# First stage of a two-block transformer kernel: the place of x in the load order, the sum of its squares, and its turned copy

## The reference, cut to what matters

```
mod = silu(c) @ w_mod + b_mod                 # six vectors of 1024; sh1, sc1 are the first two
mod_c = silu(c_ctx) @ w_mod + b_mod           # the same for the context
hx = rmsnorm(x, g_mix) * (1 + sc1) + sh1      # rmsnorm: x * rsqrt(mean(x*x) + eps) * g
hc = rmsnorm(ctx, g_mix) * (1 + csc1) + csh1
q, k, v, gates, o = hx @ w_in, and the same of hc   # four heads of 128
...                                           # chunked mLSTM over both, read-out, y
x = x + ga1 * y                               # x is needed again, by rows (tokens)
```

## Time and profile before

| | us |
|---|---|
| median of 3 runs | 1362.35 (1361.59 to 1362.79) |
| profiled execution | 1360.7 |
| its span in the profile | 1358.8 |
| PE busy | 1338.1 (98%) |
| DVE busy | 1122.8 (83%) |
| ACT busy | 779.3 (57%) |

### The profile page before, as it was taken

How to read it: one execution, slowest core, us unless ns; L and a number is a source line. 1 busy time by engine, 2 the same in 40 slices (tenths; PEclk the granted TensorE clock), 3 DMA queues, 4 the chain that set the end, 5 groups by cost and what they waited for, 6 DMA issues and landing times.

```text
span 1358.8 us, 18999 instructions
## 1 busy us (share of the span) xinstructions
PE 1338.1 (98%) x7406; PEld 1155.9 (85%) x7406; DVE 1122.8 (83%) x1659; ACT 779.3 (57%) x1145; POOL 12.9 (1%) x28
## 2 busy tenths in 40 slices
PE   8999999999999999999999999999999999999998
PEld 5988978888878888889878888888888897888886
DVE  7978787998989988879789888889887798796652
ACT  7722857676376555474475555476553757755542
POOL 0000000000000000000000000000000000000000
PEclk9999999999999999999999999999999999999999
DMA  9778445865949878777449879768889652575561
GB/s 377 285 241 302 152 157 188 297 245 199 381 185 325 298 285 330 299 259 272 165 182 329 291 287 335 292 244 319 296 283 386 218 202 93 220 264 190 192 217 33
DMA packets 64936, 343.57 MB, mean 253 GB/s; under 512 B 7408, under 2 KB 9920, under 8 KB 36688
## 3 DMA queue, kind: packets, MB, share of 16 engines
q1 hardware_dynamic: 62448, 335.35, 67.7%
q0 software_dynamic: 2224, 6.86, 1.5%
q10 hardware_dynamic: 176, 0.16, 0.0%
HBM read 341.25 MB, written 1.09 MB: 252 GB/s over the span
## 4 chain that ended last, share of the span: by engine, by line
PE 89%; DVE 4%; ACT 3%; DMA 2%; issue 1%; SPq 0%; ACTq 0%; DVEq 0%
PE bank L336 88%; DMA raw<-w_stream 2%; ACT T L836 1%; ACT rstd L738 1%; PE bank L693 1%; DVE wlo L332 1%; DVE X L930 0%; ACT whi L301 0%; PE bank L1136 0%; DVE SGC L911 0%; DVE wlo L287 0%; ACT whi L275 0%; DVE XN L871 0%; PE bank L2495 0%; DVE QR L2338 0%
## 5 line engine op out<-in xcount | busy, mean ns | idle before, releaser
L336 PE MATMUL bank<-hh,whi 128*128 128x512 f32 (+1 forms) x2160 | 484.6, 364 | 1.2 <-ACT SGC L1209 0.5
L332 DVE TENSOR_TENSOR wlo<-raw,whi 128x2048 fp32r<-128x2048 f32 x197 | 450.1, 2287 | 35.3 <-ACT whi L301 35.2
L301 ACT ACTIVATE whi<-raw 128x2048 fp32r<-128x2048 f32 x197 | 376.8, 1915 | 128.7 <-DMA raw<-w_stream 79.7
L336 PEld LDWEIGHTS bank<-hh,whi 128*128 128x128 f32 x2160 | 380.4, 189 | 60.9 <-issue 1.8
L336 PE MATMUL bank<-hh,wlo 128*128 128x256 f32 x1896 | 289.4, 283 | 0.0
L336 PEld LDWEIGHTS bank<-hh,wlo 128*128 128x128 f32 x1896 | 261.4, 191 | 8.2
L336 PE MATMUL bank<-whi,hid_hi 128*128 128x512 f32 x440 | 172.0, 391 | 0.0
L336 PE MATMUL bank<-wlo,hid_hi 128*128 128x512 f32 x440 | 171.3, 389 | 0.0
L336 PE MATMUL bank<-whi,hid_lo 128*128 128x512 f32 x440 | 171.3, 389 | 0.0
L1026 DVE SCALAR_TENSOR_TENSOR mring<-mring,con 128x1024 f32<-128x1024 f32 x107 | 130.2, 1220 | 15.7 <-DMA mring<-m_stream 15.7
L1223 ACT ACTIVATE GU<-bank 128x512 f32<-128x512 f32 x100 | 59.1, 591 | 104.8 <-PE bank L336 104.8
(11 more groups left out here) (344 smaller groups left out, 1418.6 us busy)
## 6 DMA issues: line engine op xcount, KB each, us to landing
raw<-w_stream SPq DMA_DIRECT2D x217, 1024.0 KB, 5.5
mring<-m_stream SPq DMA_DIRECT2D x139, 512.0 KB, 5.0
cb<-m_stream SPq DMA_DIRECT2D x53, 512.0 KB, 5.6
con<-gate_rows POOLq DMA_DIRECT2D x8, 512.0 KB, 7.1
raw<-w_stream SPq DMA_DIRECT2D x4, 512.0 KB, 7.4
con<-const_d SPq DMA_DIRECT2D x1, 1472.0 KB, 14.9
XF<-xT SPq DMA_DIRECT2D x1, 1024.0 KB, 13.3
XC<-ctxT SPq DMA_DIRECT2D x1, 1024.0 KB, 10.1
```

What stands on the lines that cost most here:

```text
L301: nc.scalar.activation(w_hi(c, 0, CW), raw[:, c % RAW_SLOTS], ACT.Copy).then_inc(s_hi, 1)
L332: nc.vector.tensor_tensor(w_lo(c, 0, CW), raw[:, c % RAW_SLOTS], w_hi(c, 0, CW).bitcast(f32), ALU.subtract).then_inc(s_lo, 1)
L336: return nc.tensor.matmul(out, lhsT, rhs, start=start, stop=True, skip_group_check=True)
```

## The change

x is loaded after chunk 7 instead of after chunk 3, and the 128 KB of constants before chunk 4. ACT rounds all of chunks 0 to 7, then squares x, then makes its two `mrow` copies, then rounds the first half of chunk 8, then makes rstd. DVE no longer adds the squared tiles: PE sums all eight of them, after chunk 7. Only then does PE turn `mrow`, now into bank 6, and after it all four groups of x, into banks 0, 1, 2 and 6. The filler products go. The turned x is copied to `X` later: two groups on ACT behind chunk 10's rounding, two on DVE behind the rests of chunk 9.

```
-            pe.wait_ge(s_pair, 1)
-            for j in range(2):
+            for j in range(DT):
+                if j % 4 == 0:
+                    pe.wait_ge(s_sq, j + 4)
                 ins = mm(bank[7][:, 0:SEQ], ones, SQF[:, j], j == 0)
...
-            pe.wait_ge(s_ln, 1)
+            pe.wait_ge(s_in[6], 16)
+            pe_first_stat(pe)
             for g in range(4):
...
             ins.then_inc(s_mT, 1)
-            turn_x(3)
-            pe.wait_ge(s_xc, 3)
-            pe_fill(pe, 3, ident, XF[:, 0], 4)
+            pe.wait_ge(s_in[3], 16)
+            for n in range(4):
+                if n == 3:
+                    pe.wait_ge(s_mm0, 1)
+                turn_x(n)
             pe_first_chunks(pe, U["x1"], c)
...
             dve_half_rest(dve, c, 1)
             dve_halves(dve, c + 1)
+            for n in range(2, 4):
+                dve.wait_ge(s_xt, n + 1)
+                nc.vector.tensor_copy(xrow(*GROUPS[n]), bank[X_BANKS[n]][:]).then_inc(s_xc, 1)
...
             chunks(0, 4)
-            sp.dma_start(XF[:], xT).then_inc(s_in[3], 16)
             sp.dma_start(con[:, 0:2 * P], const_d[:, 0:2 * P]).then_inc(s_in[6], 16)
             chunks(4, 8)
+            sp.dma_start(XF[:], xT).then_inc(s_in[3], 16)
```

More of the change, by code:

```diff
@@ L545, in pe_ctx_stat @@
         def pe_ctx_stat(pe):
-            pe.wait_ge(s_pair, 2)
+            pe.wait_ge(s_pair, 1)
             for j in range(2):
@@ L1370, in turned_bank @@
             return bank[3 if h < HEADS - 1 else 4]
-        X_BANKS = (4, 5, 6, 0)
+        X_BANKS = (0, 1, 2, 6)
         s_zero = sem("zeros_set")
@@ L1394, in pe_lstm @@
             for k in range(DT):
[L1395 to L1400, removed]
                 for g in range(4):
@@ L1412, in pe_lstm @@
                 for m in range(4 * g, 4 * g + 4):
-                    ins = nc.tensor.transpose(bank[7][:, SEQ + 4 * m:SEQ + 4 * m + 4], mrow[:, m * P:(m + 1) * P],
+                    ins = nc.tensor.transpose(bank[6][:, 4 * m:4 * m + 4], mrow[:, m * P:(m + 1) * P],
                                               ident[0:4, 0:4])
             ins.then_inc(s_mT, 1)
-            turn_x(3)
-            pe.wait_ge(s_xc, 3)
-            pe_fill(pe, 3, ident, XF[:, 0], 4)
+            pe.wait_ge(s_in[3], 16)
[3 more added lines that the diff above has]
+                turn_x(n)
             pe_first_chunks(pe, U["x1"], c)
@@ L1436, in pe_lstm @@
             pe.wait_ge(s_lo, c + 3)
-            pe.wait_ge(s_mm0, 1)
             gates(1, hhi, hlo)
+            pe.wait_ge(s_xc, 4)
             keys(0, 0)
@@ L1449, in values @@
                 pe_wide(pe, c + 5 + j, 4 * (j % 2), [bank[b + 4 * (j // 2)][:] for b in range(4)], his, los)
-            pe.wait_ge(s_xc, 4)
             values(0)
@@ L1559, in x_tokens @@
                 nc.scalar.activation(xrow(t, h), bank[X_BANKS[n]][:], ACT.Copy).then_inc(s_xc, 1)
-            for j in range(4):
+            for j in range(DT):
                 halves_of(j)
             act_first_squares(act)
[L1564 to L1570, removed]
             for g in (2, 3):
@@ L1573, in act_lstm @@
                 nc.scalar.activation(mrow[:, g * 512:(g + 1) * 512], bank[g][0:4], ACT.Copy).then_inc(s_mrow2, 1)
+            act_first_half(act, c)
+            act_rstd(act, N_X1, D)
             act_second_half(act, c)
@@ L1577, in act_lstm @@
             act_split(act, c + 2)
+            x_tokens(0)
+            x_tokens(1)
             act_squares(act, N_CTX, lambda j: XC[:, j], lambda j: (s_in[2], 16), False)
@@ L1582, in act_lstm @@
             act_split(act, c + 4)
-            x_tokens(3)
             act.wait_ge(s_in[4], 16)
@@ L1705, in dve_lstm @@
                 dve_halves(dve, j)
[L1706 to L1709, removed]
             for g in range(2):
@@ L1716, in dve_lstm @@
             nc.vector.tensor_reduce(CG[:, 0:2 * FIRST_MODS],
-                                    bank[7][:, SEQ:SEQ + 4 * FIRST_MODS].rearrange("p (m t) -> p m t", t=2), AX.X, ALU.add)\
+                                    bank[6][:, 0:4 * FIRST_MODS].rearrange("p (m t) -> p m t", t=2), AX.X, ALU.add)\
                 .then_inc(s_mm0, 1)
```

## The result

Over 22 runs each, the changed kernel takes 1364.04 us (1361.82 to 1366.93) and the one before 1361.88 us (1359.61 to 1366.28). The ratio is 1.0016, with a 95% interval of 1.0010 to 1.0022: 2.2 us slower (1.4 to 3.0), inside the 0.2% (2.7 us) that I called no change, though the end of the interval is not. The forecast was 1365.0 us, 2.65 us over the median then known. Two runs further down lie far off the others of their kernels and are left out of medians and ratios: one of ten of e1 (4722.94 us) and one of eight of e2 (1468.86 us, granted clock 0.85).

What follows compares the result with a forecast made beforehand. PE was taken to bound the kernel, unbroken from 43.43 us, so first-stage delays carry to the end. 1.4 + 1.2 = 2.6 us; median 1362.35 + 2.65 = 1365.0 us, own range 1364.4 to 1365.6, overall 1362.2 to 1366.8.

Steps and rivals of the forecast that it cites:

- What bounds: Whole program: PE bounds it, without a gap from 43.43 us, so a shift of that start carries to the end.
- The stream: Loads of the first stage: chunk 8 lands at 30.6 again, chunks 4 to 7 come 2.5 us sooner, x at 27.5.
- First term: First modulated tile on ACT: +1.4 us, as PE's eight sums of squares (sixteen passes) now lie on the path.
- Second term: DVE before the gates: two copies of x delay chunk 10's rest, +1.2 us, a PE gap of about 1.1 us.
- Rival A: At the gates: DVE's copies are hidden and PE does not wait for chunk 10; 1363.8 us, chance 0.11.
- Rival B: At chunk 8: early weights let rstd follow its first half on ACT without idling, DVE's copies hidden; 1362.3 us, chance 0.10.
- Rival C: Sums on PE: they run at the lower clock level, passes at double spacing, 3.3 us more; 1368.3 us, chance 0.07.
- two signs: Evidence against the lower clock on PE: spacing stayed short after an idle 0.84 us, and the granted clock was 1.00.
- Rival D: Loads: x lands beside chunk 8, later than its place in line; at 30.6, +1.5 us, 1366.5 us, chance 0.06.
- slower by over 0.2%: Whole run: over 2.7 us slower, chance 0.39, from 0.28 of the forecast's own spread with C and D.

Runs made afterwards that it cites:

- e1: The changed kernel with DVE's two copies of the turned x made by ACT behind chunk 11's rounding; 1364.29 us, ratio 1.0014 to the kernel before.
- e2: The changed kernel with DVE adding the squares pairwise, so PE sums four tiles instead of eight; 1364.02 us, ratio 1.0014 to the kernel before.
- the first experiment: The same run as e1: DVE's two copies of x given to ACT in the changed kernel; 1364.29 us, ratio 1.0014 to the kernel before.
- e10: The kernel before with only ACT's list reordered, its load order kept; 1361.94 us, ratio 0.9999 to the kernel before.
- e7: The changed kernel with ACT's two copies of x moved behind chunk 11's rounding, DVE's two left; one run, gates 20.78 us after chunk 8.

## Why the prediction was right

- **What bounds, and that the shift is carried on: right.** 2.35 us at the gates, 2.35 us at 221 us.
- **The stream: right.** x at 27.58 (27.5 said), chunk 8 again at 30.6, chunk 6 at 22.47 (22.5), and PE at the sums at 29.30 (29.4).
- **First term: right, a little large.** 1.26 us measured, 1.4 said (the working gives 33.05 + 0.9 - 32.52 = 1.43). A pass cost 0.216 us (0.217), the sums ended 0.1 us sooner since PE began 0.1 sooner, and ACT took 0.83 us from the start of L562 to its next instruction, not 0.9. The doubled sums showed that every pass is on the path.
- **Second term: right in size, incomplete in cause.** 1.09 us measured, 1.2 said; two copies on DVE did take 1.20 us, and 0.1 of it filled the wait for ACT's squares that stood there before. The "gap of about 1.1 us" in PE was counted from the start that the gates could have had (49.56 + 0.76 = 50.32, by the kernel before); the profile's 0.82 us counts from the end of the last pass (50.59). The prediction said that ACT's two copies leave the context's squares done at 47.1, "still ahead of the pair sums". That held, with 0.1 us to spare, and it meant more than I wrote: this was a second hold of nearly the same length, the one that had been last before. Asking what would be late next if DVE's copies were not there would have shown it, and the expectation of the first experiment would not have failed.
- **Rival A** (copies hidden) fell at the gap of 0.82 us. **Rival B**: its bound held. With four sums ACT went from 30.42 to 32.19 without idle time, 0.14 us sooner against chunk 8 than before, and nothing more was to be had until ACT's list was reordered, which it had taken as given. **Rival C**: the passes were 0.216 us apart. Of the two signs that the prediction named, only this spacing decides. The granted clock reads 1.00 at the sums, but it reads 1.00 from 8 to 12 us too, where the products of 512 columns start 0.43 us apart, against 0.23 later. That early stretch, the two ahead of the sums and that of the sums (span, busy time per engine, then PEclk):

```profile
8.00:12.00 4.00, 3.65 (x8) 2.48 (x8) 2.68 (x4) 2.23 (x3) 0.00 (x0) 1.00 1.01 426
24.00:28.00 4.00, 3.84 (x15) 2.22 (x14) 4.00 (x4) 2.79 (x4) 0.00 (x0) 1.00 1.04 422
28.00:29.30 1.30, 1.30 (x6) 0.86 (x5) 1.30 (x3) 1.30 (x2) 0.00 (x0) 1.00 0.99 410
29.30:33.00 3.70, 3.70 (x20) 3.00 (x18) 1.31 (x2) 2.34 (x5) 0.00 (x0) 1.00 1.01 423
```

  By the rule of the Trainium skill ("TensorE: Matmul & The Clock Gate", "HAM oscillation — how this bites in real kernels") this rival was not the likely one, as the prediction had it: the page's case is a wait for the next load that is longer than the burst of products before it. The trace shows no such wait here: PE was busy for 3.84 of the 4 us from 24 to 28, and its longest wait between chunks from 12 us to the sums was 0.50 us. **Rival D**: x landed in its turn.
- **The time.** 2.65 us was said, 2.2 (1.4 to 3.0) measured, 2.35 in the trace. The absolute figure was another 0.5 us high because the median of the first three runs (1362.35) lay above that of 22 (1361.88). The time alone would not have told the forecast from rival A: 2.2 us lies between A's 1.4 and the 2.65 said, and the interval reaches both. It is the gap at the gates that rules A out.
- **Chances.** The terms given for "slower by over 0.2%" add up to 0.28 + 0.07 + 0.06 = 0.41 with C and D taken whole, not 0.39.

## What to carry to other kernels

Work that runs under a stream of loads is free only there. Moving an operand to the end of the stream puts everything made of it on the path, so its reduction has to be short by then: eight float32 sums on TensorE cost 1.3 us where four, with two additions on another engine, cost nothing. Before a copy is put on an engine, ask not only what is queued behind it but which other engine's list, moved by the same edit, ends 0.1 us behind it: a hold that is hidden by another shows no wait in the profile until that one is taken away. And a shift of 2 us in a run of 1360 is read in the trace from a fixed event (here the landing of a load), not from two spans.

## What was not expected of the hardware

The wait for the same load on the path, some 1060 us into the program, took 6.20, 8.13, 8.22, 7.20, 6.91, 6.61, 5.62, 7.06, 6.82, 6.96, 7.44 and 6.82 us in the twelve profiles (before, changed, e1 to e10), with no relation to the edit: e1 with 8.22 and e7 with 6.82 differ only in how x is copied at 45 us. Waits of 6.1 to 7.7 us for weights at about 372, 563 and 867 us, and of 7.4 to 8.8 us for `m_stream` at 359 to 364, lay on the path in some of the profiles and not in others. Between the two fixed places (at about 221 and 1185 us) the twelve profiles take 960.3 to 964.2 us: 3.9 us, nearly twice the effect of the change. And the landing of chunk 8, at the end of 30 us of unbroken transfers, varied by 0.3 us (30.33 to 30.61).
